# Picking an expert pair's tokens: long products with the one-hot matrix as weights, then copied and transposed, in place of short products that give the transposed tokens directly

## The reference

```python
h = jax.nn.silu(jnp.einsum('nd,edf->nef', xt, w_gate)) * jnp.einsum('nd,edf->nef', xt, w_up)
h = h * combine.astype(h.dtype)[:, :, None]
y = jnp.einsum('nef,efd->nd', h, w_down)
```

## Time and profile before

| what | value |
|---|---|
| median of 3 runs | 1168.8 us (1168.37 to 1170.16) |
| the profiled execution's own time | 1168.16 us |
| its span, first to last instruction | 1166.3 us |
| TensorE matmul busy | 1105.4 us (95%) |
| TensorE weight load busy | 654.0 us (56%) |
| VectorE / ScalarE / GpSimd busy | 414.0 / 229.2 / 128.3 us |
| moved by DMA | 321.27 MB, mean 275 GB/s |
| chain that ended last | 80% TensorE, 11% DMA, 4% VectorE |

### The profile page before, as it was taken

One profiled execution on the slowest core, in us unless ns is written; L12 is line 12 of the kernel. 1 busy time (PEld: TensorE's weight loads), 2 busy tenths in 40 slices (PEclk: granted clock), 3 DMA queues, 4 the chain that ended last, 5 costly groups with the idle time before them and its releaser, 6 DMA issues.

```text
span 1166.3 us, 19793 instructions
## 1 busy us (share of the span) xinstructions
PE 1105.4 (95%) x8488; PEld 654.0 (56%) x8488; DVE 414.0 (36%) x1059; ACT 229.2 (20%) x531; POOL 128.3 (11%) x226
## 2 busy tenths in 40 slices
PE   4999999999899999999998899998999899999996
PEld 1666666666444576666654444444555656666562
DVE  2155656556712341000112655306863320000114
ACT  3111011011211321111111411115642411111110
POOL 0344434334100000000002000000000000000003
PEclk9999999999999999999999899999999999999999
DMA  9985444446842579999999920079770789999996
GB/s 346 291 292 149 136 146 146 146 146 217 338 187 89 180 270 423 411 428 427 424 427 348 368 102 1 18 258 371 263 281 18 253 353 418 429 426 424 425 418 227
DMA packets 102464, 321.27 MB, mean 275 GB/s; under 512 B 4048, under 2 KB 39168, under 8 KB 87008
## 3 DMA queue, kind: packets, MB, share of 16 engines
q1 hardware_dynamic: 93872, 298.05, 66.9%
q0 software_dynamic: 3248, 10.87, 2.8%
q10 hardware_dynamic: 5248, 10.98, 2.4%
HBM read 305.73 MB, written 14.16 MB: 274 GB/s over the span
## 4 chain that ended last, share of the span: by engine, by line
PE 80%; DMA 11%; DVE 4%; SPq 2%; issue 2%; ACT 1%; POOL 1%; POOLq 0%; ACTq 0%; DVEq 0%
PE bank L788 17%; PE bank L941 11%; PE bank L1181 11%; PE bank L811 7%; PE bank L678 7%; PE bank L777 6%; DMA ring<-in_moe_w_down 5%; PE bank L950 4%; PE bank L1067 4%; DMA ring<-in_w_ada 4%; PE bank L573 3%; PE bank L966 2%; PE bank L657 1%; DMA ring<-expert_rows,moe_row 1%; PE bank L664 1%
## 5 line engine op out<-in xcount | busy, mean ns | idle before, releaser
L788 PE MATMUL bank<-ring,xn 128*64 128x256 f32 x1472 | 163.5, 380 | 0.9 <-DMA ring<-in_moe_w_up 0.9
L788 PEld LDWEIGHTS bank<-ring,xn 128*64 128x64 f32 x1472 | 105.0, 137 | 61.4 <-issue 9.5
L941 PE MATMUL bank<-uT,ring 128*128 128x384 f32 x384 | 135.0, 496 | 0.0
L1181 PE MATMUL bank<-ring,uT 128*128 128x512 f32 x288 | 129.5, 603 | 4.3 <-DMA ring<-in_attn_w_qkv 2.7
L1869 DVE TENSOR_TENSOR moe_hh<-xn,bank 128x256 f32<-128x256 f32 x32 | 13.5, 421 | 291.7 <-ACT xn L1336 291.6
L811 PE MATMUL bank<-ring,xn 128*64 128x512 f32 x384 | 106.7, 596 | 0.9 <-ACT xn L1342 0.9
L941 PEld LDWEIGHTS bank<-uT,ring 128*128 128x128 f32 x384 | 69.2, 190 | 41.4 <-issue 1.1
L1181 PEld LDWEIGHTS bank<-ring,uT 128*128 128x128 f32 x288 | 54.1, 193 | 68.2 <-issue 64.1
L678 PE MATMUL bank<-ring,uT 128*128 128x512 f32 x192 | 84.1, 592 | 0.0
L777 PE MATMUL bank<-moe_g,moe_h 128*128 128x128 f32 x672 | 83.7, 282 | 0.5 <-DVE moe_g L1759 0.5
L777 PEld LDWEIGHTS bank<-moe_g,moe_h 128*128 128x128 f32 x672 | 79.9, 197 | 5.6 <-issue 5.6
(11 more groups left out here) (293 smaller groups left out, 1328.2 us busy)
## 6 DMA issues: line engine op xcount, KB each, us to landing
ring<-in_w_ada SPq DMA_DIRECT2D x24, 2048.0 KB, 12.1
ring<-in_moe_w_up SPq DMA_DIRECT2D x24, 2048.0 KB, 18.7
ring<-in_moe_w_gate SPq DMA_DIRECT2D x22, 2048.0 KB, 19.5
ring<-in_moe_w_down SPq DMA_DIRECT2D x21, 2048.0 KB, 19.9
ring<-in_hgrn_w_in SPq DMA_DIRECT2D x32, 512.0 KB, 6.9
moe_ring<-in_moe_w_gate SPq DMA_DIRECT2D x8, 2048.0 KB, 19.5
moe_ring<-in_moe_w_up SPq DMA_DIRECT2D x8, 2048.0 KB, 23.3
moe_ring<-in_moe_w_down SPq DMA_DIRECT2D x7, 2048.0 KB, 21.0
```

The lines of the kernel that those rows point to most:

```text
L788: last = mm(bank[2 + e][64 * g:64 * g + 64, 256 * part:256 * part + 256], m["xe"][:, k, 64 * e:64 * e + 64], w[k][:, 256 * g:256 * g + 256 ...
L941: last = mm(to[:, 0:TOK], w[:, k, f, :], uT[:, k, :], start=(k == 0), stop=(k == KC - 1))
L1181: last = mm(bank[b % 2][:, :], uT[:, k, t * P:(t + 1) * P], cols(slot)[:, k, :], start=(k == 0), stop=(k == KC - 1))
```

## The change

For the pairs that are not fetched (0 and 2 to 7) the gather is done in two steps. `pick_rows(half, i)`: three products with the one-hot matrix as weights and 512 features of the tokens as the moving operand give 128 slots x 512 features in the bank; ScalarE (half 0) and VectorE (half 1) copy that to `m["own"][:, 1, :]` (`picked`). Then `gather` transposes, as it does for the fetched pair, for all pairs. The products for the next pair lie between the gate and up products of this pair (after the second and the third of the four), the transpositions where the gather was. The fetch of pair 1 now waits until pair 0's transpositions have been done, since it writes to the same place. In `collect` only further passes wait for something else.

```diff
--- before.py
+++ after.py
@@ -55,7 +55,7 @@
 LAST_MM = 4 + T
 WRITES = PAIRS - 1
 FETCHED = 1
-GATHERS = 2 * PAIRS + FETCHED
+GATHERS = 4 * PAIRS - FETCHED
 ONEHOTS = PAIRS + FETCHED
 ROWS_IN = (32, 48, 32)
 RING = 8
@@ -384,13 +384,26 @@
             return p * ONEHOTS + (2 * i + 1)
-        def tokens_summed(p, i):
-            return p * GATHERS + 2 * i
+        def tokens_summed(p):
+            return p * GATHERS + 4
+        def fetched(i):
+            return 1 <= i <= FETCHED
+        def gathers_before(i):
+            return 0 if i == 0 else 4 * i + FETCHED if i == 1 else 4 * i - FETCHED
+        def rows_picked(p, i, half):
+            return p * GATHERS + (gathers_before(i) + half + 1)
         def pair_gathered(p, i, half):
-            return p * GATHERS + (2 * i + half + 1 + (FETCHED if i or half else 0))
+            return p * GATHERS + (gathers_before(i) + (0 if fetched(i) else 2) + half + 1
+                                  + (FETCHED if i == 0 and half == 1 else 0))
         def passes(eng, n):
@@ -761,29 +774,31 @@
                                   start=(t == 0), stop=(t == T - 1))
                     last.then_inc(s["gathered"], 1)
-                def gather(half, i):
+                def pick_rows(half, i):
                     if half == 0:
-                        if 1 <= i <= FETCHED:
-                            pe.wait_ge(s[f"rows{i}"], at_pass[0] * ROWS_IN[i] + 16)
-                        else:
-                            pe.wait_ge(s["onehot"], onehots_made(at_pass[0], i))
+                        pe.wait_ge(s["onehot"], onehots_made(at_pass[0], i))
+                    for t in range(T):
+                        last = mm(bank[half][:, :], m["g"][:, t, :, :], m["h"][:, t, 512 * half:512 * half + 512],
+                                  start=(t == 0), stop=(t == T - 1))
+                    last.then_inc(s["gathered"], 1)
+                def gather(half, i, it):
+                    if not fetched(i):
+                        pe.wait_ge((s["xe_act"], s["xe_dve"])[half], it * 2 + 1)
+                    elif half == 0:
+                        pe.wait_ge(s[f"rows{i}"], at_pass[0] * ROWS_IN[i] + 16)
                     for k in range(4):
-                        if 1 <= i <= FETCHED:
-                            here = slice((4 * half + k) * P, (4 * half + k + 1) * P)
-                            last = nc.tensor.transpose(bank[half][:, k * P:(k + 1) * P], m["own"][:, i, here], ident)
-                            continue
-                        for t in range(T):
-                            last = mm(bank[half][:, k * P:(k + 1) * P],
-                                      m["h"][:, t, (4 * half + k) * P:(4 * half + k + 1) * P],
-                                      m["g"][:, t, :, :], start=(t == 0), stop=(t == T - 1))
+                        here = slice((4 * half + k) * P, (4 * half + k + 1) * P)
+                        last = nc.tensor.transpose(bank[half][:, k * P:(k + 1) * P], m["own"][:, 1, here], ident)
                     last.then_inc(s["gathered"], 1)
                 def gate_up(i, e, part, it):
                     w = weights_in(i, 2 * e + part)
                     for k in range(KC):
                         if e == 0 and part == 0 and k == 4:
-                            pe.wait_ge(s["xe_dve"], it + 1)
+                            pe.wait_ge(s["xe_dve"], it * 2 + 2)
                         for g in range(2):
                             last = mm(bank[2 + e][64 * g:64 * g + 64, 256 * part:256 * part + 256],
                                       m["xe"][:, k, 64 * e:64 * e + 64],
@@ -842,7 +857,8 @@
                 def body(i, it, first, last):
-                    pe.wait_ge(s["xe_act"], it + 1)
+                    pe.wait_ge(s["xe_act"], it * 2 + 2)
+                    picking = not last and not fetched(i + 1)
                     gating = i == GATE_PAIR and isinstance(it, int)
                     gate_up(i, 0, 0, it)
@@ -850,6 +866,8 @@
                         pe.wait_ge(s["passes_ready"], 1)
                         gate(n, m["diag"], 1, 0, 6)
                     gate_up(i, 0, 1, it)
+                    if picking:
+                        pick_rows(0, i + 1)
                     if gating:
                         gate(n, m["diag"], 1, 1, 6)
                     if last:
@@ -858,11 +876,13 @@
                             turned = nc.tensor.transpose(bank[0][:, t * P:(t + 1) * P], m["gw"][:, t, :, :], ident)
                         turned.then_inc(s["last_mm"], 1)
                     gate_up(i, 1, 0, it)
+                    if picking:
+                        pick_rows(1, i + 1)
                     if gating:
                         gate(n, m["diag"], 1, 2, 6)
                     gate_up(i, 1, 1, it)
                     if not last:
-                        gather(0, i + 1)
+                        gather(0, i + 1, it + 1)
                     if gating:
                         gate(n, m["diag"], 1, 3, 6)
                     pe.wait_ge(s["h_ready"], it * 2 + 2)
@@ -874,7 +894,7 @@
                                 m["hh"][:, e, j * P:(j + 1) * P] if last else every_other, ident)
                     turned.then_inc(s["hT_done"], 1)
                     if not last:
-                        gather(1, i + 1)
+                        gather(1, i + 1, it + 1)
                     pe.wait_ge(s["hT_ready"], it + 1)
                     down(i, it)
@@ -882,9 +902,11 @@
                 def before(p):
                     at_pass[0] = p
-                    gather(0, 0)
+                    pick_rows(0, 0)
+                    pick_rows(1, 0)
+                    gather(0, 0, p * PAIRS)
                     tokens_of(1)
-                    gather(1, 0)
+                    gather(1, 0, p * PAIRS)
                 def after(p):
@@ -1314,12 +1336,18 @@
                 def rows(i):
                     act.wait_ge(s["gathered"], pair_gathered(at_pass[0], i, 0))
-                    A(m["xe"][:, 0:4, :], bank[0][:, :], ACT.Copy).then_inc(s["xe_act"], 1)
+                    A(m["xe"][:, 0:4, :], bank[0][:, :], ACT.Copy).then_inc(s["xe_act"], 2 if fetched(i) else 1)
+                def picked(i):
+                    act.wait_ge(s["gathered"], rows_picked(at_pass[0], i, 0))
+                    A(m["own"][:, 1, 0:512], bank[0][:, :], ACT.Copy).then_inc(s["xe_act"], 1)
                 at_pass = [0]
                 def before(p):
                     at_pass[0] = p
+                    picked(0)
                     rows(0)
                 def body(i, it, first, last):
@@ -1334,6 +1362,8 @@
                             A(m["wc"][:, :], bank[0][:, 0:TOK], ACT.Copy).then_inc(s["wc_ready"], 1)
                         act.wait_ge(*expert_used(n, i, 2 * e + 1, at_pass[0]))
                         A(m["sg"][:, e, :], bank[2 + e][:, 0:256], ACT.Silu).then_inc(s["silu"], 1)
+                        if e == 0 and not last and not fetched(i + 1):
+                            picked(i + 1)
                     if not last:
                         rows(i + 1)
                     if gating:
@@ -1816,13 +1846,19 @@
                 def tokens_of(i):
-                    dve.wait_ge(s["gathered"], tokens_summed(at_pass[0], i))
+                    dve.wait_ge(s["gathered"], tokens_summed(at_pass[0]))
                     v.tensor_copy(m["idx"][:, i - 1:i], bank[4][:, 0:1]).then_inc(s["onehot"], 1)
                 def rows(i):
                     dve.wait_ge(s["gathered"], pair_gathered(at_pass[0], i, 1))
-                    v.tensor_copy(m["xe"][:, 4:8, :], bank[1][:, :].rearrange("p (k n) -> p k n", k=4)).then_inc(s["xe_dve"], 1)
+                    v.tensor_copy(m["xe"][:, 4:8, :], bank[1][:, :].rearrange("p (k n) -> p k n", k=4))\
+                        .then_inc(s["xe_dve"], 2 if fetched(i) else 1)
+                def picked(i):
+                    dve.wait_ge(s["gathered"], rows_picked(at_pass[0], i, 1))
+                    v.tensor_copy(m["own"][:, 1, 512:1024], bank[1][:, :]).then_inc(s["xe_dve"], 1)
                 at_pass = [0]
@@ -2283,16 +2322,20 @@
                     for i in range(1, FETCHED + 1):
                         pool.wait_ge(s["onehot"], token_known(p, i))
+                        pool.wait_ge(s["gathered"], pair_gathered(p, 0, 1))
                         g.tensor_tensor(m["flag"][:, 1:2], ones[:, 0:1], ones[:, 0:1], ALU.mult)
                         pool.drain()
-                        g.indirect_dma_start(m["own"][:, i, :], None, token_table[n],
+                        g.indirect_dma_start(m["own"][:, 1, :], None, token_table[n],
                                              bass.IndirectOffsetOnAxis(ap=m["idx"][:, i - 1:i], axis=0))\
                             .then_inc(s[f"rows{i}"], 16)
                 def collect(p):
                     pool.wait_ge(s["oe_out"], p * (16 * WRITES) + 16 * WRITES)
-                    pool.wait_ge(s["down_half"], p * 32 + 32)
+                    if isinstance(p, int):
```

(3 more changed lines are left out.)

## The result

The changed kernel takes **1196.92 us** in the median of 4 runs (1191.43 to 1198.22) against 1168.59 before (4 runs): a ratio of 1.0231, 95% interval 1.0198 to 1.0264, so 28.3 us slower, where 1195.5 (1186 to 1203) had been forecast. Its profiled execution took 1196.99 us with a span of 1195.1, 28.8 above the span before, and its mean granted clock was 0.986 against 0.991. Two later sets of runs, each with its own runs of the kernel before, gave 1.0260 (1.0220 to 1.0299) and 1.0272 (1.0239 to 1.0306), 30.2 and 30.3 us.

A forecast was written before the change was run, and what follows sets the result against it. TensorE and DMA both full, added TensorE time paid nearly whole: 0.5 + 11.6 + 2.7 = 14.8 us a layer, less end waits 13.6 and 13.7, together +27.3 on 1168.2, so 1195.5 us, range 1186 to 1203.

The forecast's parts named there:

- What bounds the kernel: Expert stage: TensorE and DMA both full, ending within a microsecond; TensorE time saved worth nothing, time added paid nearly whole.
- Lost cover: Pairs 1 to 5: moved passes no longer cover TensorE's waits around the hidden values' transpositions; net +2.32 us a pair.
- streaming: Gather work per pair: 12 long passes at 5.15 us replace 48 short at 5.36, saving 0.2; eight transpositions add 0.9.
- Breaks: Picks inside gate and up products switch TensorE's array mode twice more a pair, 0.34 us each.
- The lower bound: Picks laid in free of breaks, waits a little shorter: 1.62 us a pair instead of 2.32, 1188 us.
- Pair 6: Pair with gate products: picks 5.14, wait for copy and diagonal about 1.5, end block saves 3.9; +2.7 us.
- The start: Stage start: 12 passes for 48 (-0.2), eight transpositions (+0.9); pair 0's gate products some 0.5 us later.
- DMA stays full: Loads issued at most 19 us later against a 31 us queue, so DMA stays full and last landings come only 0.5 us later.
- The end: Last pair: its DMA wait goes (0.86 and 0.79 us by layer), and a 0.33 us wait for result rows, counted as -0.3.
- A (hidden behind the DMA): Rival: last matrices' landing and `collect` set the stage's end, only the later start counts; 1169 us, chance 4%.
- B (long passes cheap): Rival: 512-wide passes cost much less than their columns, about 0.196 us each; kernel 6 us faster, 1162 us, chance 2%.
- C (the clock falls in the new waits): Rival: TensorE's clock drops after each pair's new idle times, 1.3 us in each of 12 pairs; +16, 1211 us, chance 4%.

The follow-up runs named there:

- the short products: The kernel before, its 48 short gather passes a pair laid inside the gate and up products, where the changed kernel has its long ones: 1209.50 us (1.0334).
- the one-block run: The changed kernel with both picks of a pair in one block after the first expert's products: 1193.98 us (1.0199).
- the added passes: The kernel before with six more 512-column passes, result unused, after down in pairs 1 to 5 of each layer: 1207.63 us (1.0316).
- the cover given back: The changed kernel with the picks where the gather had been and the picked rows' transpositions between the halves of down: 1179.73 us (1.0071).

## Why the prediction was right, point by point

- **What bounds the kernel.** "Time taken off TensorE would be worth nothing; time added is paid nearly whole": shown from both sides, 5 us for 50 taken away, 37.6 for 29 added.
- **Lost cover, +2.32 a pair.** 2.33 measured (29.19 - 26.86). The terms behind it hold: place 2.54 (1.94 of it the uncovered hand-overs, most of the rest the breaks, see the short products), streaming -0.21. Taking pair 0's end block whole, with its transpositions and both waits, was the right reading; the 0.9 us for transpositions, counted by themselves under streaming, is not in the net of a pair.
- **Breaks, 0.34 each.** Shown by the one-block run. The lower bound, no break, is excluded. The rule of the Trainium skill that a change of tiling mode drains TensorE (TensorEngine Tiling (Array Packing), Key Properties) agrees with that 0.34; no run tells the drain from another cost of the switch.
- **Pair 6, +2.7.** 33.95 - 31.34 = 2.61 in the profile, with a wait of 1.38 us for the diagonal, where 1.5 was taken.
- **The start, +0.5.** 0.86 measured. The prediction's own terms, -0.2 and +0.9, already make 0.7. Twelve passes took 6.73 us from 414.76 to 421.49 instead of the 6.5 that 5.15 and the 1.3 of low clock make, and two hand-overs more.
- **DMA stays full; the result fetches come late but in time.** Both held in the first profile: GpSimd's wait now ends at 633.59 with pair 6's write, issued at 627.32 and landed within 6.3 us, less than the 10.5 of the earlier trace rows. But the prediction looked only at when the fetched rows are needed. That the fetches would be issued beside the last pair's products, it did not price. In the profiles of both later sets this overlap came with 4 to 5 us lost in each layer, a term that stands in no sum of the prediction; the first profile was spared. So the forecast fits the first runs better (28.3 us) than the later sets (30.2 and 30.3), and that is luck.
- **The end.** The waits named went; from pair 6's down to the last pair's it is 1.08 us less in layer 0 (24.96 to 23.88), where 0.86 was counted. A third wait went that I had not counted: 2.66 us for the first mixer weights of layer 1. The term -0.3 was -1.3 and -0.9. The 0.33 us behind that term had been read in layer 1 alone. There 0.40 of the 0.94 lie between the last pair's down and the first product with the result rows, and the rest behind VectorE's last sum.
- **What was not in the sum** are 3.1 us outside the stages, 1.6 ahead of layer 0's stage and 1.5 between the two stages. The first can't be the change's work; for the second it isn't shown either way. Both are of the size by which profiles of one kernel differ: the first gather product of the kernel before comes at 413.14 us in one profile and at 415.99 in the other. One of the four runs had a granted clock of 0.992 and took 1191.43 us. That the forecast came within 1.5 us owes something to the two misses, +3.1 and -1.6, working against each other.
- **Rivals.** A (hidden behind the DMA): the added passes refute it. B (long passes cheap): the picks' passes are 0.43 us apart, 3.8 times the 0.112 of the short ones. The 1.6 ratio that the Trainium skill gives (TensorE: Matmul & The Clock Gate, Back-to-back issue gap) is not seen here; these are float32 passes. C (the clock falls in the new waits): 1.00 over 430 to 640 in the changed kernel. In the run with short products inside, which has the same waits, the down after the wait took 1.7 us more in two of the six pairs of each layer, with a clock of 0.83 over 467 to 477. So the case exists, but not in each pair, and the changed kernel's profiles don't show it in pairs 1 to 6.

## What to carry to other kernels

Work on an engine has a value as cover: before moving products away from where they stand, read what the chain would run through in their place. Here nearly six microseconds of products hid two of hand-overs, and the same products elsewhere cost 2.5 us a pair (1.9 for the hand-overs, the rest mostly for two breaks in the products they were laid into), while the new form itself saved 0.2. When two resources finish together, check the sign of slack on both sides by one kernel with time added and one with work left out, before tuning either. A fetch that becomes ready earlier than its consumer may be worth holding back.

## What was not expected of the hardware

In all six profiles of the experiments in which GpSimd's six indirect transfers were issued beside the products of the last pair's second expert, the Silu after these products came only 2.2 to 2.5 us after the sixth was issued, and the sixteen passes of down that follow took 5.2 to 5.8 us in layer 0 instead of 3.65, with a granted clock of 0.79 over 8 us in the changed kernel. Together that was 4 to 5 us a layer in the changed kernel; holding the transfers back recovered 5.6 us in the median. The two parts are not one: with the cover given back, only the first two transfers were issued ahead of that Silu, which came with the end of its products (632.63), and the passes still took 5.35 us, with a clock of 0.79 over 634 to 642. The first profile of the changed kernel showed neither part, with nearly the same overlap. The cause stays open.
